# Expert rows gathered from memory by GpSimd, and expert results combined into x by TensorE

## The reference

```python
e_logits = (xf @ w_re + b_re).reshape(n_tok, N_GROUPS, EXPERTS_PER_GROUP)
chosen = take_along_axis(e_logits, g_top[:, None, None], axis=1)[:, 0]
top_vals, top_idx = lax.top_k(chosen, 2)              # 2 of the 8 experts of one group
weights = p_g[:, None] * softmax(top_vals)
# rows of one expert are collected into chunks:
ys = (silu(xc @ w_gate[e]) * (xc @ w_up[e])) @ w_down[e]
out = segment_sum(ys * row_w[:, None], row_tok, num_segments=n_tok)   # added to x
```

## Time and profile before

| | us |
|---|---|
| time, median of 3 runs | 1690.32 (1688.18 to 1690.77) |
| the profiled execution | 1688.36 |
| its span, first to last instruction | 1686.6 |

### The profile page before, as it was taken

The page is one execution under the profiler, slowest core; times in us unless marked ns, Lnnn a source line. Parts: engine busy times, 40 slices in busy tenths (PEclk is TensorE's granted clock), DMA queues, the critical chain, the costliest instruction groups (busy, mean ns, idle before and its releaser), DMA issues. The chain is left out here.

```text
span 1686.6 us, 18294 instructions
## 1 busy us (share of the span) xinstructions
PE 1564.3 (93%) x6924; PEld 737.3 (44%) x6924; DVE 587.2 (35%) x1587; ACT 387.5 (23%) x790; POOL 86.2 (5%) x93
## 2 busy tenths in 40 slices
PE   8999988999999999949999999996999999999992
PEld 4444444444444443325554455554444444444340
DVE  2111255222222221255264587545322222222225
ACT  2000131111111111132243478522111111111112
POOL 0000010000000000000000000011000000000000
PEclk9999998999999999979999899997999999999996
DMA  6261218999999999964310300035999999999994
GB/s 200 75 275 49 67 74 349 425 426 425 425 426 426 425 426 426 418 197 131 100 51 1 150 2 1 17 150 198 396 426 426 425 426 426 425 426 426 426 403 169
DMA packets 110101, 469.48 MB, mean 278 GB/s; under 512 B 26416, under 2 KB 53040, under 8 KB 59312
## 3 DMA queue, kind: packets, MB, share of 16 engines
q1 hardware_dynamic: 104800, 459.75, 66.9%
q0 software_dynamic: 5200, 8.40, 1.3%
HBM read 457.63 MB, written 19.14 MB: 283 GB/s over the span
## 5 line engine op out<-in xcount | busy, mean ns | idle before, releaser
L816 PE MATMUL ps<-raw,e_xT 128*64 128x512 f32 x2080 | 462.3, 593 | 22.4 <-DMA raw<-in_expert_w_up 21.7
L816 PEld LDWEIGHTS ps<-raw,e_xT 128*64 128x64 f32 x2080 | 152.1, 137 | 320.7 <-issue 319.3
L917 DVE TENSOR_TENSOR e_sg_hid<-e_sg_hid,ps 64x512 f32<-64x512 f32 x65 | 44.3, 681 | 567.0 <-ACT e_sg_hid L863 567.0
L840 PE MATMUL ps<-raw,e_hT 128*64 128x512 f32 x1040 | 237.5, 598 | 0.0
L406 PE MATMUL ps<-c_hT,raw 128*128 128x512 f32 x384 | 165.0, 592 | 0.2 <-ACT c_hT L351 0.2
L868 ACT ACTIVATE e_ysb<-ps 64x512 f32<-64x512 f32 x130 | 77.0, 592 | 289.3 <-PE ps L840 288.5
L863 ACT ACTIVATE e_sg_hid<-ps 64x512 f32<-64x512 f32 x65 | 38.6, 593 | 399.0 <-PE ps L816 399.0
L784 PE MATMUL ps<-m_xhi,e_pick 128*128 128x512 f32 x276 | 118.9, 431 | 9.3 <-DVE e_pick L886 9.3
L840 PEld LDWEIGHTS ps<-raw,e_hT 128*64 128x64 f32 x1040 | 68.9, 136 | 122.3 <-issue 111.4
L1467 PE MATMUL ps<-a_spare,raw 128*128 128x512 f32 x256 | 113.8, 601 | 1.5 <-ACT a_spare L1174 1.5
L406 PEld LDWEIGHTS ps<-c_hT,raw 128*128 128x128 f32 x384 | 72.9, 190 | 91.7 <-issue 91.1
(11 more groups left out here) (226 smaller groups left out, 1390.1 us busy)
## 6 DMA issues: line engine op xcount, KB each, us to landing
raw<-in_expert_w_gate SPq DMA_DIRECT2D x130, 1024.0 KB, 23.6
raw<-in_expert_w_up SPq DMA_DIRECT2D x130, 1024.0 KB, 24.7
raw<-in_expert_w_down SPq DMA_DIRECT2D x130, 1024.0 KB, 24.5
raw<-in_conv_w_in SPq DMA_DIRECT2D x12, 1024.0 KB, 9.6
k_rows<-pairs_y SPq DMA_DIRECT2D x6, 1024.0 KB, 9.8
raw<-in_w_kv SPq DMA_DIRECT2D x6, 1024.0 KB, 7.2
raw<-in_conv_w_out SPq DMA_DIRECT2D x1, 4096.0 KB, 18.2
raw<-in_attn_w_in SPq DMA_DIRECT2D x4, 1024.0 KB, 5.5
```

What stands on the lines that cost most here:

```text
L816: mm = pe.matmul(ps_gu[C - C * i:2 * C - C * i, :], xT[:, q % 2, k, u * C:(u + 1) * C], ring(m, L, p)[:, kk * F:(kk + 1) * F], start=(k == ...
L840: mm = pe.matmul(ps_y[c % 2][n * C:(n + 1) * C, :], hT[:, 2 * h + kk, :], ring(m, L, p)[:, kk * D + n * 512:kk * D + (n + 1) * 512], start ...
L917: dve.tensor_tensor(hid, sg, ps_gu[0:C, :], ALU.mult).then_inc(s_hid, 1)
```

## The change

- The normed rows of x are written to memory (`rows_x`) by SyncE, tile by tile. Both `vector_normed` and the router's norm now write features in the experts' order, and read x in steps of 8 floats.
- Behind `slots`, `table` computes with DVE and eight small products which token stands at each place of each chunk. GpSimd gathers the rows of a chunk pair, 128 places, from memory by these indices (empty places point out of bounds). The high and low parts, `pick` for the gather, its products and their evictions go.
- The results are multiplied by their weight (a table by 16 small products in chunk 0) as ScalarE evicts them, as a rounded high part `yhi`, and DVE makes the low part `ylo`. Two chunks lie on 128 partitions. One pair later TensorE multiplies them with a 0/1 matrix that spreads the rows over the tokens (four tiles of 128 tokens, two in each chunk's step), and DVE adds the sums to x. The scatter, `pairs_y`, its reload and `Combine` go.
- An overflow chunk is combined by itself, tile by tile, right behind its down product; the last pair comes after it, interleaved with the norm that follows. The last norm and the output move into `experts` 1; the norm before `shared_kv` moves into `experts` 0, as do the first loads of that stage, and its transposes come in `shared_kv` without waits between them.
- `vector_tail` runs first in DVE's part of `experts`, ahead of the eviction of the first transposes. GpSimd's first two gathers are in the block of the router, and SyncE issues pieces 12 to 15 in the block behind it, as before.

```diff
     def vector_normed(self, dve, xn, t):
-        dve.tensor_scalar(xn[:, t, :], self.m.x[:, t, :], self.m.rstd[:, self.n, t:t + 1], None,
+        dve.tensor_scalar(by_k_out(xn[:, t, :]), by_k(self.m.x[:, t, :]), self.m.rstd[:, self.n, t:t + 1], None,
                           ALU.mult).then_inc(self.xn, 1)
 
-    def tensor(self, pe, xn):
+    def tensor(self, pe, xn, waiting=True):
         for t in range(NT):
-            pe.wait_ge(self.xn, t + 1)
+            if waiting:
+                pe.wait_ge(self.xn, t + 1)
             for k in range(NK):
-                tr = pe.transpose(self.m.ps[k][:, t * P:(t + 1) * P], xn[:, t, k::NK], self.m.ident[:])
+                tr = pe.transpose(self.m.ps[k][:, t * P:(t + 1) * P], xn[:, t, k * P:(k + 1) * P], self.m.ident[:])
...
     def sync_ring(self, sp):
 
-        sp.wait_ge(self.s_o, 2 * NT)
-        prefetch(sp, self.m, self.L, range(8, 12))
+        for t in range(NT):
+            if t == NT - 1:
+                sp.wait_ge(self.s_o, 2 * NT)
+                prefetch(sp, self.m, self.L, range(8, 12))
+            sp.wait_ge(self.s_xn, t + 1)
+            sp.dma_start(self.m.rows_x[self.L][t * P:(t + 1) * P, :], self.xn[:, t, :]).then_inc(self.s_out, 16)
...
+        pe.wait_ge(self.s_hot, 1)
+        self.tensor_table(pe, m.ps[4], self.rhot[:], self.ctok[:], 1).then_inc(self.s_tok, 1)
+
+    def tensor_table(self, pe, bank, rows, cols, halves):
+
+        for i in range(NTK):
+            for u in range(halves):
+                mm = pe.matmul(bank[u * C:(u + 1) * C, 0:NCH], rows[:, i, :], cols[:, i, :],
+                               start=(i == 0), stop=(i == NTK - 1))
+        return mm
...
-    def low_parts(self, pool):
-        for t in range(NT):
-            pool.wait_ge(self.s_xhi, t + 1)
-            pool.tensor_tensor(self.m.xlo[:, t], by_k(self.xn[:, t, :]), self.m.xhi[:, t].bitcast(F32),
-                               ALU.subtract).then_inc(self.s_xlo, 1)
+    def first_rows(self, pool):
+
+        pool.wait_ge(self.s_o, 1)
+        pool.memset(self.rows[:], 0.0).then_inc(self.s_zero, 1)
+        pool.wait_ge(self.s_zero, 1)
+        pool.wait_ge(self.s_idx, 2)
+        pool.wait_ge(self.s_out, 16 * NT)
+        for q in range(2):
+            self.gather(pool, q)
+
+    def gather(self, pool, q):
+
+        pool.indirect_dma_start(out=self.rows[:, q % 2, :], out_offset=None, in_=self.m.rows_x[self.L][:, :],
+                                in_offset=bass.IndirectOffsetOnAxis(ap=self.idx[:, q:q + 1], axis=0),
+                                bounds_check=S - 1, oob_is_err=False).then_inc(self.s_rows[q % 2], 16)
...
+        def table():
+            slot = m.slot[:].rearrange("p t k -> p (t k)")
+            col, row = self.pos[:, 0], self.pos[:, 1]
+            own.step(dve.tensor_scalar(col, slot, 0.5 - C / 2, MAGIC * C, ALU.add, ALU.add))
+            own.step(dve.tensor_scalar(col, col, MAGIC * C, None, ALU.subtract))
+            own.step(dve.tensor_tensor(row, slot, col, ALU.subtract))
+            dve.tensor_tensor(self.chot[:], self.col[:].unsqueeze(1).broadcast_to([P, NTK, NCH]),
+                              col.unsqueeze(2).broadcast_to([P, NTK, NCH]), ALU.is_equal).then_inc(self.s_own, 1)
+            own.n += 1
+            own.step(dve.tensor_tensor(self.rhot[:], m.iota[:, 0:C].unsqueeze(1).broadcast_to([P, NTK, C]),
+                                       row.unsqueeze(2).broadcast_to([P, NTK, C]), ALU.is_equal))
+            dve.tensor_tensor(self.ctok[:], self.chot[:], m.token[:].rearrange("p t k -> p (t k)").unsqueeze(2)
+                              .broadcast_to([P, NTK, NCH]), ALU.mult).then_inc(self.s_hot, 1)
+            found = m.ps[4][0:C, 0:NCH]
+            far = self.far[0:C, :]
+            dve.wait_ge(self.s_tok, 1)
+            own.step(dve.tensor_scalar(far, found, 0.5, FAR, ALU.is_lt, ALU.mult))
+            for u in range(PAIR):
+                dve.scalar_tensor_tensor(out=self.idx[u * C:(u + 1) * C, :], in0=found[:, u::PAIR], scalar=-1.0,
+                                         in1=far[:, u::PAIR], op0=ALU.add, op1=ALU.add).then_inc(self.s_idx, 1)
+            for u in range(2):
+                own.step(dve.tensor_scalar(self.tok[u * C:(u + 1) * C, :], found, 1.0, None, ALU.subtract))
...
+        dve.tensor_tensor(self.cwts[:], self.chot[:], m.wts[:].rearrange("p t k -> p (t k)").unsqueeze(2)
+                          .broadcast_to([P, NTK, NCH]), ALU.mult).then_inc(self.s_cw, 1)
...
-        def pe_gather(pe, n):
...
         def pe_turn(pe, n):
 
+            pe.wait_ge(r.s_rows[q % 2], 16 * (q // 2 + 1))
+            wait(pe, s_xev, n)
+                tr = pe.transpose(ps_t[:, k * GS:(k + 1) * GS], rows[:, q % 2, (h * HK + k) * P:(h * HK + k + 1) * P],
+                                  m.ident[:])
...
+        def pe_combine(pe, chunks, t, banks, done):
+
+            for c in chunks:
+                pe.wait_ge(s_pick, c + 1)
+                pe.wait_ge(s_ylo, c + 1)
+            c = chunks[-1]
+            half = slice(0, P) if len(chunks) == PAIR else half_of(c)
+            for n in range(2):
+                for part in (yhi, ylo):
+                    mm = pe.matmul(banks[n][:], pick[half, pick_place(c), t * P:(t + 1) * P],
+                                   part[half, y_place(c), n * 512:(n + 1) * 512], start=(part is yhi), stop=(part is ylo))
+                mm.then_inc(done, 1)
...
+            q = c // PAIR - 1
+            if PAIR <= c < E:
+                for t in (2 * (c % 2), 2 * (c % 2) + 1):
+                    pe_tile(pe, (PAIR * q, PAIR * q + 1), t, 4 * q + t)
+            if c == 0:
+                pe.wait_ge(r.s_cw, 1)
+                r.tensor_table(pe, ps_c[0][0], r.rhot[:].bitcast(F32), r.cwts[:], 2).then_inc(s_wt, 1)
             pe_transpose(pe, c)
-            pe_turn(pe, c + PAIR)
+            if c + PAIR < NCH:
+                pe_turn(pe, c + PAIR)
             pe_down(pe, c)
-
-        def act_rows(act, n):
-
-            wait(act, s_rg, n + 1)
-            wait(act, s_xt, n - 1)
-            act.activation(rows[:, n % 2].rearrange("p k q -> p (k q)"), ps_r[n % 2][:], ACT.Copy).then_inc(s_rev, 1)
+            if c >= E:
+                for t in range(NT):
+                    pe_tile(pe, (c,), t, LAST + 4 * (c - E) + t)
+                pe.wait_ge(s_add, 2 * (LAST + 4 * (c - E) + 4))
...
-            act_rows(act, c + PAIR)
             wait(act, s_used, c * NPIECE + 6)
-            wait(act, s_st[c % 2], c // 2 * 16)
+            if c == 0:
+                act.wait_ge(s_wtab, 1)
+            if 4 <= c < E:
+                act.wait_ge(s_comb, 8 * (c // 2 - 1))
+            if c >= E:
+                act.wait_ge(s_comb, 2 * LAST + 8 * max(c - E - 1, 0))
             for n in range(2):
-                y = act.activation(ysb[:, c % 2, n * 512:(n + 1) * 512], ps_y[c % 2][n * C:(n + 1) * C, :], ACT.Copy)
-            y.then_inc(s_yev, 1)
+                y = act.activation(yhi[half_of(c), y_place(c), n * 512:(n + 1) * 512], ps_y[n * C:(n + 1) * C, :], ACT.Copy,
+                                   scale=wtab[n * C:(n + 1) * C, c:c + 1])
+            y.then_inc(s_yhi, 1)
...
+            q = c // PAIR + 2
+            if c % PAIR == 0 and q < NCH // PAIR:
+                pool.wait_ge(s_xt, 2 * q - 2)
+                r.gather(pool, q)
...
+        def dve_low(dve, c):
+
+            dve.wait_ge(s_yhi, c + 1)
+            for n in range(2):
+                cols = slice(n * 512, (n + 1) * 512)
+                y = dve.scalar_tensor_tensor(out=ylo[half_of(c), y_place(c), cols], in0=ps_y[n * C:(n + 1) * C, :],
+                                             scalar=wtab[n * C:(n + 1) * C, c:c + 1],
+                                             in1=yhi[half_of(c), y_place(c), cols].bitcast(F32),
+                                             op0=ALU.mult, op1=ALU.subtract)
+            y.then_inc(s_ylo, 1)
...
+            if 0 < c < E:
+                dve_low(dve, c - 1)
             wait(dve, s_sg, c + 1)
             wait(dve, s_ht, c)
             dve.tensor_tensor(hid, sg, ps_gu[0:C, :], ALU.mult).then_inc(s_hid, 1)
+            if c == 0:
+                dve.wait_ge(s_wt, 1)
+                dve.tensor_copy(wtab[:], ps_c[0][0][:, 0:NCH]).then_inc(s_wtab, 1)
+                dve.wait_ge(s_wtab, 1)
+            q, t = c // PAIR - 1, 2 * (c % 2)
+            if PAIR <= c < E:
+                dve_add(dve, t, 4 * q + t)
             wait(dve, s_ht, c + 1)
             wait(dve, s_used, c * NPIECE)
             dve.tensor_copy(hT[:].rearrange("p k c -> p (k c)"), ps_h[:, 0:KF * C]).then_inc(s_hev, 1)
+            if c + PAIR < NCH:
+                dve_turned(dve, c + PAIR)
+            if PAIR <= c < E:
+                dve_add(dve, t + 1, 4 * q + t + 1)
+            if c < E and c % PAIR:
+                for i in (c - 1, c):
+                    dve_pick(dve, i)
+            if c >= E:
+                dve_pick(dve, c)
+                dve_low(dve, c)
```

(35 more changed lines are left out.)

366 lines of the change are left out of this document (145 added, 221 removed).

## The result

The changed kernel takes 1708.4 us (median of 4 runs, 1706.7 to 1710.6), the kernel before, run beside it, 1689.25 us (1687.9 to 1690.8). The ratio is 1.0114, 95% interval 1.0096 to 1.0131: slower by 19 us, where 1685.4 was predicted with a range up to 1697. The profiled execution has a span of 1707.1 us, 20.5 more than before.

A forecast was written before the change was run, and what follows sets the result against it. Bound by the DMA weight stream, 15.07 us a chunk. +1.8 + 2.7 - 3.4 + 2.1 - 8.1 = -4.9 from the profiled 1688.36 gave 1683.5, and with the median 1.96 us longer 1685.4; range 1677 to 1697 us.

The forecast's parts named there:

- What bounds the kernel: Expert stages: the DMA stream sets the pace at 15.07 us a chunk; TensorE's work below that is hidden.
- Rival C: Expert stage: DVE's additions hold the copy to `e_hT`, TensorE falls behind the loads; 1692 us at 0.1 us above; 8%.
- Start of layer 0, +1.8: Four `vector_normed` operations ahead of the first projection, slowed by strided reads to 1.2 us, +0.45 each: +1.8 us.
- Router's norm: Router's last tile, ahead of the slots: its strided norm had no cost in the forecast, +1.07 us twice in rival B.
- rival B: Norms at layer 0's start and end and in the router: every strided one costs double, +10.1 us, 1695.5; 14%.
- GpSimd's hold on DVE, -2.47: Router: without GpSimd's subtraction a DVE operation takes 0.24 us instead of 2.71; slots come 2.47 us earlier.
- Hand-over, +2.7 and +2.1: Router to first gate product: pieces 12 to 15 issued 5.1 us later, less existing idle: +2.7 in layer 0, +2.1 in layer 1.
- the block's end adds 0.5: End of the router's block, behind the two gathers: 0.5 us until SyncE issues pieces 12 to 15.
- Inside the stage, 0: Expert stage: equal bytes, and 14.1 us a chunk of work hidden under 15.07 us of loads: no change.
- Layer 0's end, -3.4: Last down product to next stage's first projection: 27.4 us instead of 30.4, down product 0.2 to 0.6 earlier: -3.4 us.
- Layer 1's end, -8.1: Last gate product done to the span's end: 32.4 us instead of 40.5, a gain of 8.1 us.
- D: Gathers from memory: empty places aren't skipped, 4.2 MB more a layer, 9.9 us each, 1705 us; 4%.

The follow-up runs named there:

- e5: The changed kernel with 192 bytes of padding ahead of the weight ring's second part, which then starts at byte 86016, a multiple of 512: 1696.2 us.
- e6: The kernel before with its 32 bytes of slots allocated ahead of the weight ring's second part, which then starts at byte 84512: 1702.3 us, ratio 1.008.

## Why the prediction was wrong, point by point

- **What bounds the kernel** was right: a stage ends with its stream (wait of 0.98 us ahead of the last gate product), and DVE's extra work hid under it (13.70 us a chunk for TensorE, where 14.1 were forecast). Rival C didn't happen.
- **Start of layer 0, +1.8**: right, +1.9, 1150 ns an operation where 1.2 us were taken.
- **Router's norm**: the step that failed here was costing it at nothing outside rival B. With two strided inputs DVE took 2078 ns instead of 1284. So rival B's price held for this form, where it counts once a layer (0.8 us), and not for the norm with one strided input. The prediction read "Door 1: The DMA port swizzle" of the Trainium skill's SBUF — State Buffer as ScalarE's 2057 ns for every norm. The passage gives no price. The trace agrees for the form with two strided inputs alone; with one it shows 1150, which isn't free either.
- **GpSimd's hold on DVE, -2.47**: right. The 16 operations at L649 take 242 ns on the mean, none 2.71 us.
- **Hand-over, +2.7 and +2.1**: the failed step is "the block's end adds 0.5". It added 3.2 us, since it waits for the gathers' rows. The table (4.2 us for 4.6, whose own terms add up to 4.5) and the gathers (1.01 and 0.99 for 1.1 each) were sized right. SyncE's four pieces came 8.8 and 8.6 us later, not 5.1: of the 3.5 or more that were missing 2.7 is the block's end, 0.8 the norm. The first gate product came 15.9 us behind the slots instead of 12.8, and its price for the clock's lower level was sized right (9.06 and 9.44 us for 7.09 before, 2.4 forecast). A landing of 3.2 us taken from a scatter's row was near (4.1), but the prediction hid it behind vector_tail and overlooked that SyncE, whose loads need nothing of it, waits at the same barrier.
- **Inside the stage, 0**: the largest failure, a term put at nothing because the loads hid TensorE's and DVE's work. "The bytes are equal" was true, and the rate didn't stay: 426 to 421 GB/s, 12 us of the 19 (e5, e6). In the kernel's code the constant `iota` grows from 128 to 512 columns ahead of the ring; nothing in the prediction looked at addresses, and no row of the trace before gives the price.
- **Layer 0's end, -3.4**: right, -3.5: 27.3 us for 27.4 from the down product on, and 0.4 ahead of it.
- **Layer 1's end, -8.1**: the mechanism was right, three terms too small: the way out of the branches 4.1 us for 0.6, the four tiles of the overflow chunk 7.0 for 5.6 (TensorE at the clock's lower level, 0.43 us from product to product, paces them, not DVE), the first combine behind the branches 1.2 for 0.5. Together 5.6 of the 5.7 missing.
- **Rivals**: D is out (8.40 MB on the queue). The slower outcome had 29%, but by mechanisms of which only a small part happened (B's norm with two strided inputs, 0.8 us a layer), and the measured 1708.4 lies 11 us above the range. Neither the address nor the barrier was a rival.

## What to carry to other kernels

When a kernel is bound by a stream into SBUF, look at where its buffers lie before and after a change that grows anything allocated ahead of them, and pin the address (512 bytes was enough here). Before costing a block's end at a semaphore, ask which engine issued indirect DMAs in it: every engine waited for them here. And where a gather's latency is on a path, what is queued beside it is part of its price; order the queue so that it finds it empty, and fill only what lands before it starts.
